# Matmuls of 512 columns that read the second copy of x, each split into two of 256 columns

## The reference

```python
D_MODEL = 1024
SEQ = 512
D_FF = ((8 * D_MODEL // 3 + 255) // 256) * 256

def swiglu(h, w_gu, w_down):
    gate, up = jnp.split(h @ w_gu, 2, axis=-1)
    return (jax.nn.silu(gate) * up) @ w_down
...
        x = x + 0.5 * swiglu(rmsnorm(x, ffn1_norm[l]), ffn1_w_gu[l], ffn1_w_down[l])
        x = x + token_mixing(rmsnorm(x, mix_norm[l]), w_in[l], lower_bounds[l],
                             hg_norm[l], conv_w[l], conv_norm[l], w_out[l])
        x = x + cross_attention(rmsnorm(x, xa_norm[l]), rmsnorm(mem, mem_norm[l]),
                                xa_wq[l], xa_wkv[l], xa_wo[l])
        x = x + 0.5 * swiglu(rmsnorm(x, ffn2_norm[l]), ffn2_w_gu[l], ffn2_w_down[l])
    return rmsnorm(x, final_norm)
```

## Time and profile before

| | us |
|---|---|
| median of three runs | 1103.45 |
| the three runs | 1101.84, 1103.45, 1112.93 |
| the profiled execution | 1100.7 |
| its span on the core | 1098.9 |

### The profile page before, as it was taken

One profiled execution on the slowest core, in us unless ns is written; L12 is line 12 of the kernel. 1 busy time (PEld: TensorE's weight loads), 2 busy tenths in 40 slices (PEclk: granted clock), 3 DMA queues, 4 the chain that ended last, 5 costly groups with the idle time before them and its releaser, 6 DMA issues.

```text
span 1098.9 us, 17317 instructions
## 1 busy us (share of the span) xinstructions
PE 1083.4 (99%) x6328; PEld 951.3 (87%) x6328; DVE 638.4 (58%) x944; ACT 525.8 (48%) x738; POOL 441.0 (40%) x546
## 2 busy tenths in 40 slices
PE   9999999999999999999999999999999999999997
PEld 7889999988888888787789888888899999888886
DVE  7887777572223668978477134466977777531012
ACT  6445555542223554664366443354555555633231
POOL 0000000486665445346448883163010000585550
PEclk9999999999999999999999999999999999999999
DMA  7277775333333121222323442122576675333212
GB/s 244 78 213 198 192 201 172 116 115 99 112 104 106 58 96 58 77 77 78 119 67 121 164 162 78 39 77 77 168 209 186 185 190 172 116 115 113 98 58 77
DMA packets 49458, 136.89 MB, mean 125 GB/s; under 512 B 4736, under 2 KB 11008, under 8 KB 49280
## 3 DMA queue, kind: packets, MB, share of 16 engines
q1 hardware_dynamic: 43888, 118.90, 31.5%
q0 software_dynamic: 4320, 15.73, 8.6%
q10 hardware_dynamic: 1200, 1.57, 0.4%
HBM read 134.09 MB, written 2.10 MB: 124 GB/s over the span
## 4 chain that ended last, share of the span: by engine, by line
PE 52%; POOL 25%; issue 21%; DVE 1%; POOLq 0%; DMA 0%; ACT 0%; DVEq 0%; SPq 0%; ACTq 0%
POOL wl L528 25%; PE bank L1629 8%; PE bank L1631 8%; PE bank L1630 8%; PE bank L1734 4%; PE bank L1735 4%; PE bank L1736 4%; PE score L1734 3%; PE score L1735 3%; PE score L1736 3%; PE o_bank L1734 1%; PE o_bank L1735 1%; PE o_bank L1736 1%; PE bank L1690 1%; PE bank L1694 0%
## 5 line engine op out<-in xcount | busy, mean ns | idle before, releaser
L528 POOL TENSOR_TENSOR wl<-raw,wh 128x256 fp32r<-128x256 f32 x512 | 414.7, 843 | 314.6 <-ACT wh L562 271.3
L562 ACT ACTIVATE wh<-raw 128x1024 fp32r<-128x1024 f32 x120 | 125.7, 1053 | 137.7 <-PE bank L1631 135.6
L1629 PE MATMUL bank<-xh,wh 128*128 128x512 f32 x456 | 183.0, 401 | 0.5 <-DVE V L1509 0.5
L1631 PE MATMUL bank<-xh,wl 128*128 128x512 f32 x456 | 178.5, 391 | 0.0
L1630 PE MATMUL bank<-xl,wh 128*128 128x512 f32 x456 | 178.4, 391 | 0.0
L542 POOL DMA_DIRECT2D raw<-w_all x30 | 26.1, 869 | 317.8 <-DMA raw<-w_all 317.8
L1629 PE MATMUL bank<-zr,wh 128*128 128x512 f32 (+1 forms) x374 | 141.0, 377 | 0.0
L1630 PE MATMUL bank<-zr,wh 128*128 128x512 f32 (+1 forms) x374 | 140.8, 377 | 0.0
L1631 PE MATMUL bank<-zr,wl 128*128 128x512 f32 (+1 forms) x374 | 140.8, 377 | 0.0
L1013 DVE SCALAR_TENSOR_TENSOR x<-bank,x 128x512 f32<-128x512 f32 (+1 forms) x31 | 21.3, 687 | 160.5 <-PE bank L1631 160.1
L1629 PEld LDWEIGHTS bank<-xh,wh 128*128 128x128 f32 x456 | 85.6, 188 | 20.3 <-issue 2.4
(11 more groups left out here) (325 smaller groups left out, 2554.4 us busy)
## 6 DMA issues: line engine op xcount, KB each, us to landing
raw<-w_all SPq DMA_DIRECT2D x200, 512.0 KB, 3.3
raw<-w_all POOLq DMA_DIRECT2D x30, 512.0 KB, 5.4
zf<-w_all SPq DMA_DIRECT2D x30, 256.0 KB, 4.4
x<-x_t SPq DMA_DIRECT2D x8, 256.0 KB, 6.2
out_t<-x SPq DMA_DIRECT2D x8, 256.0 KB, 2.6
raw<-w_all SPq DMA_DIRECT2D x6, 256.0 KB, 6.1
memf<-mem_t ACTq DMA_DIRECT2D x1, 1024.0 KB, 5.5
raw<-w_all ACTq DMA_DIRECT2D x2, 256.0 KB, 4.1
```

The source lines that it names most:

```text
L528: ins = nc.gpsimd.tensor_tensor(wl[:, slot, two], raw[:, slot, two], wh[:, slot, two].bitcast(f32), SUB)
L562: nc.scalar.activation(wh[:, slot, :], raw[:, slot, :], ACT.Copy).then_inc(hi_ready, 1)
L1629: nc.tensor.matmul(out_, a[0], b_[0], start=first, stop=False)
L1631: return nc.tensor.matmul(out_, a[1], b_[0], start=False, stop=last)
```

## The change

`group` calls a new function, `product_halves`, where its source is the second copy of x. For each of the three products it issues two matmuls of 256 columns, one after the other, on the left and the right half of the 512 columns, into the left and the right half of the same bank. The weights are the same in both, and each has its own weight load. Only the very first of a unit starts the bank anew. Eight units in each of the two FFN blocks are reached: four in front of the pairs and four behind them.

```diff
+            def product_halves(out_, a, b_, first, last):
+
+                for i, j, start, stop in ((0, 0, first, False), (0, 1, False, False), (1, 0, False, last)):
+                    for h in range(2):
+                        ins = nc.tensor.matmul(out_[:, HALVES[h]], a[i], b_[j][:, HALVES[h]], start=start and h == 0, stop=stop,
+                                               skip_group_check=True)
+                return ins
+
...
-                    last = product(bank[g % 4][:, 0:cols_], wpair(slot, 128 * k, 128 * k + 128),
+                    multiply = product_halves if src[0] is xh_apart else product
+                    last = multiply(bank[g % 4][:, 0:cols_], wpair(slot, 128 * k, 128 * k + 128),
                                    (src[0][:, k, :], src[1][:, k, :]), k == 0, k == KC - 1)
```

## The result

The kernel became 1% slower, not 0.2% faster. The changed kernel takes 1113.94 us (median of 16 runs, 1113.19 to 1115.72), the kernel before 1102.1 us (16 runs beside them, 1101.26 to 1112.93). The ratio on record is 1.0104, with a 95% interval from 1.0095 to 1.0114; the two medians alone give 1.0107. The profiled execution took 1113.34 us with a span of 1111.4, which is 12.5 us more span than before.

A forecast was written before the change was run, and what follows sets the result against it. TensorE, busy for 99%, was taken as the bound; 16 units at 0.16 us less each gave 2.56 us, so profiled execution 1100.7 - 2.56 = 1098.1 us. Forecast time 1100.3 us, range 1097.0 to 1106.0.

The forecast's parts named there:

- The step that failed: In the 16 split units, each new 256-column matmul was priced at 113.3 ns, as read in the pairs.
- The table of four cells: TensorE matmul distances by start byte and width: 128/512 226.7 ns, 128/256 120.0, 64/512 233.3, 64/256 113.3.
- The halves are dear: Rival, 16 units: 256-column matmuls cost 120.0 ns, deciding from 116.7 ns on; kernel 2.56 us slower; chance 0.05.
- One half is dear: Rival, split units: each second matmul pays 6.7 ns, two halves cost 233.3 ns; change 0.0 us; chance 0.04.
- The gain is late elsewhere: Rival, units in front of the pairs: a wait takes back their gain, 1.28 us remain; chance 0.04.
- The gain of 0.16 us a unit: Each of the 16 split units was to take 5.44 us in place of 5.60.
- the prediction's estimate of 0.96 us: By the page's 2.5 ns for each matmul, 384 more matmuls would cost 0.96 us; the sum didn't use it.
- The written signs: Expected in the timeline: a unit 5.44 us, four in front 21.76, second block's first pair some 1.9 us before 794.05.

The follow-up runs named there:

- e9: Kernel before, nothing split, but the last unit in front of the pairs reads the first copy of x (start 128); 1112.51 us, one run.
- e2: Changed kernel with only the four units behind the pairs split in each block; 1100.37 us, ratio 0.9984 to the kernel before.
- e5: Changed kernel with the first front unit's first step of k, three matmuls, kept 512 wide at start 64; 1099.99 us, ratio 0.998.
- e7: Changed kernel plus one unused 512-column matmul on the second copy (start 64) ahead of each block's first pair; 1104.11 us, one run.
- e3: Changed kernel with the first of the four front units kept 512 wide in each block; 1099.28 us, ratio 0.9968 to the kernel before.
- e11: e12 plus one unused 512-column matmul at start 64 ahead of the key projection; 1098.94 us, ratio 0.9968 to the kernel before.
- e12: e5 with the buffers of the memory tokens and keys shifted to start 64 modulo 256; 1098.59 us, ratio 0.9961 to the kernel before.
- e8: Kernel before, nothing split, with the pairs reading at start 128 and the last front unit at start 64; 1118.02 us, one run.

## Why the prediction was wrong

**The step that failed** is "Their operands are the halves of the second copy, start 64, with weights from `wh` and `wl`, which is what the pairs read the earlier trace rows, so I take 113.3 ns". The 113.3 ns was a reading of the pairs behind wide matmuls at start 64, and the sum took it for a property of place and width. The new run begins behind wide matmuls at start 128, and e9 shows that this alone makes 117.8 ns of it, e2, e5 and e7 that the other entry gives 113.3. The table of four cells had no column for what led in, and its cell for start 64 and 256 columns had been read behind one entry only.

**The term that was absent** is the larger one. The sum counted the 16 units and left the pairs' price untouched. The split joins units in front, pairs and units behind into one run of 256 columns, and its pace holds to the run's end: 192 + 1176 + 192 = 1560 matmuls in the first block and 1728 in the second. So 2520 matmuls that the diff doesn't touch pay 4.44 ns each, 11.2 of the 12.5 us. The 16 units, forecast at -2.56 us, came to +0.9, and the other 0.5 us lie ahead of the change.

**The rivals.** *The halves are dear* had the sign, but neither the mechanism nor the size: its place was the 16 units, its price 120.0 ns and its sum 2.56 us. The measured 117.8 even lies on its side of the 116.7 ns from which it was to decide; e2 shows that the halves need not pay it. *One half is dear* falls with the same run, 5.44 us for a unit of 48. *The gain is late elsewhere* didn't come up, since no wait row changed.

**What was right.** Nothing became late: eight of the nine rows of waits stand as they were, and there is no new one. Between the blocks all shifts as a whole, 543.44 us against 543.43, only in the other direction. The gain of 0.16 us a unit exists: e2 has it behind the pairs, and e3, e5, e11 and e12 in front as well. The cell "start 128, 256 columns: 120.0 ns" held when the pairs were moved there (e8). No price for a matmul as such shows in these runs: in e2 48 halves took 5.44 us where the earlier trace rows have 5.44 for 24 wide ones on the first copy. The Trainium skill, page "TensorE: Matmul & The Clock Gate", section "Back-to-back issue gap", states its 2.5 ns for a matmul by itself and gives other figures for a stream of weight loads and matmuls, so the prediction's estimate of 0.96 us used the formula where the page doesn't.

**The written signs.** A unit at 5.65 us, not 5.44; the four in front 22.61, not 21.76; the first pair of the second block at 800.42, not 792.1. "The prediction is wrong if the distance isn't decided by the start byte and the width" is what happened.

Open is why an entry sets a pace. Shown is only what sets it: 24 wide matmuls at start 128 bring the slow one and one doesn't; numbers in between weren't tried. The start byte of the wide float32r matmuls and their distance (226.7 ns at 128, 233.3 at 64) go together in all runs, so which of the two counts isn't told apart. Start 64 alone isn't enough for the fast pace: the sum of squares that ended it in e11 reads `acc`, which the program places at byte 118080, 64 modulo 256, but in plain float32.

## What to carry to other kernels

The price of an instruction that is read in one neighbourhood belongs to that neighbourhood: when a change joins or parts streams on the bounding engine, put a term into the sum for the work on either side that the diff doesn't touch. Where TensorE is busy for 99% before and after, only distances between starts, or matmuls counted in equal windows, show such a loss. Here it is cheap to lead a long run of 256-column float32r matmuls in with one wide float32r matmul on an operand at start 64, provided that the run reads at start 64 too, and nothing of another kind stands inside it.

## What the runs showed of the hardware

On these float32r operands, with a weight load each, a matmul of 256 columns has three paces at the full clock: 113.3, 117.8 and 120.0 ns. The middle one held for over 180 us in the changed kernel (from 50.64 to 234.37 us), a stretch in which TensorE has no row of waits. Mean lengths of weight loads from 85 to 185 us go with them (columns: busy time, mean ns). The changed kernel, at 117.8 ns:

```profile
L1745 PEld LDWEIGHTS bank<-xh,wl 128*128 128x128 f32 x43 | 8.3, 192 | 0.0
L1744 PEld LDWEIGHTS bank<-xl,wh 128*128 128x128 f32 x43 | 8.1, 188 | 0.0
L1743 PEld LDWEIGHTS bank<-xh,wh 128*128 128x128 f32 x42 | 7.9, 188 | 0.0
```

Before, at 113.3 ns, the same groups read 188 throughout; in e8, at 120.0, 192 throughout. In the middle pace one load in three is a long one, and in the pairs it is that of a product's third matmul. The split units show that it doesn't go by the product, which has six matmuls there. Loads of the changed kernel from 57 to 72 us:

```profile
L1640 PEld LDWEIGHTS bank<-xh,wh 128*128 128x128 f32 x44 | 6.7, 188 | 0.0
L1640 PEld LDWEIGHTS bank<-xl,wh 128*128 128x128 f32 x43 | 6.6, 190 | 0.0
```

The two loads of `bank<-xl,wh` are the third and the fourth of the six, and in order of time the third is the long one; `bank<-xh,wl`, the fifth and the sixth, also reads 190, and there the sixth is long. So it is each third load of the run. 117.8 is also the mean of one matmul at 113.3 and two at 120.0 ns, but the starts that the trace records lie 117 to 119 ns apart from one matmul to the next, so single matmuls at 113.3 and at 120.0 aren't seen. How the middle pace comes about was not shown.
